# Norm chains of a two-layer diffusion trunk: additions and low parts on GpSimd, one function table for Ln and Exp, weight pieces split in halves

## The reference, cut to what matters

```python
def _rms_norm(x, g):
    xf = x.astype(jnp.float32)
    y = xf * lax.rsqrt(jnp.mean(xf * xf, axis=-1, keepdims=True) + EPS)
    return (y * g.astype(jnp.float32)).astype(x.dtype)

def _modulate(h, shift, scale):
    return h * (1 + scale) + shift
...
        h = _modulate(_rms_norm(x, norm_g[0]), sh1, sc1)
        hc = _modulate(_rms_norm(ctx, norm_g[0]), csh1, csc1)
...
        x = x + g1 * _rms_norm(y, norm_g[1])
        h2 = _modulate(_rms_norm(x, norm_g[2]), sh2, sc2)
        x = x + g2 * _rms_norm(ffn(h2), norm_g[3])
```

## Time and profile before

| | us |
|---|---|
| median of three runs | 1876.46 |
| lowest and highest | 1873.37 and 1878.36 |
| the profiled execution, its own time | 1877.49 |
| its span, first to last instruction | 1875.7 |
| TensorE, VectorE, ScalarE, GpSimd busy | 1744.5, 1080.5, 951.6, 0.2 |
| expert stage, first matmul to last | about 1032 to 1855 |

### The profile page before, as it was taken

The page is one execution under the profiler, slowest core; times in us unless marked ns, Lnnn a source line. Parts: engine busy times, 40 slices in busy tenths (PEclk is TensorE's granted clock), DMA queues, the critical chain, the costliest instruction groups (busy, mean ns, idle before and its releaser), DMA issues. The chain is left out here.

```text
span 1875.7 us, 22323 instructions
## 1 busy us (share of the span) xinstructions
PE 1744.5 (93%) x8560; PEld 1365.7 (73%) x8560; DVE 1080.5 (58%) x1076; ACT 951.6 (51%) x1037; POOL 0.2 (0%) x4
## 2 busy tenths in 40 slices
PE   6898999889999999699775999999999999999995
PEld 3685357458888788379564788888888888888884
DVE  2341332232222333453634798888888989899895
ACT  3513332352222222542454576767677777777774
POOL 0000000000000000000000000000000000000000
PEclk8898999889999999889986899999999999999997
DMA  7424374452222222132023698989899999999870
GB/s 274 194 90 170 106 263 160 180 198 90 94 108 90 90 95 107 37 107 79 40 94 131 245 367 327 367 324 368 339 353 346 348 348 345 353 340 375 320 307 24
DMA packets 56655, 403.05 MB, mean 215 GB/s; under 512 B 6288, under 2 KB 7568, under 8 KB 7952
## 3 DMA queue, kind: packets, MB, share of 16 engines
q1 hardware_dynamic: 56592, 402.17, 56.8%
HBM read 401.10 MB, written 1.05 MB: 214 GB/s over the span
## 5 line engine op out<-in xcount | busy, mean ns | idle before, releaser
L1114 DVE TENSOR_TENSOR wl<-raw,wh 128x2048 fp32r<-128x2048 f32 x269 | 615.7, 2292 | 101.1 <-ACT wh L670 100.9
L670 ACT ACTIVATE wh<-raw 128x2048 fp32r<-128x2048 f32 x269 | 515.3, 1917 | 150.9 <-PE ps L1198 150.9
L1196 PE MATMUL ps<-wh,ah 128*128 128x512 f32 (+1 forms) x808 | 314.2, 389 | 1.4 <-issue 1.4
L1198 PE MATMUL ps<-wh,al 128*128 128x512 f32 (+1 forms) x808 | 306.4, 379 | 0.0
L1196 PE MATMUL ps<-ah,wh 128*128 128x512 f32 (+1 forms) x736 | 285.5, 388 | 22.2 <-DVE al L764 14.3
L1197 PE MATMUL ps<-wl,ah 128*128 128x512 f32 (+1 forms) x808 | 305.3, 378 | 0.0
L1197 PE MATMUL ps<-al,wh 128*128 128x512 f32 (+1 forms) x736 | 277.9, 378 | 0.0
L1198 PE MATMUL ps<-ah,wl 128*128 128x512 f32 (+1 forms) x736 | 277.5, 377 | 0.0
L739 DVE TENSOR_TENSOR wl<-raw,wh 128x2048 fp32r<-128x2048 f32 x60 | 137.4, 2291 | 145.6 <-ACT wh L370 145.6
L1196 PEld LDWEIGHTS ps<-ah,wh 128*128 128x128 f32 x736 | 142.6, 194 | 58.2 <-issue 13.4
L1198 PEld LDWEIGHTS ps<-wh,al 128*128 128x128 f32 x808 | 152.6, 189 | 29.4
(11 more groups left out here) (217 smaller groups left out, 1727.6 us busy)
## 6 DMA issues: line engine op xcount, KB each, us to landing
raw<-in_w SPq DMA_DIRECT2D x377, 1024.0 KB, 4.8
x<-in_x SPq DMA_DIRECT2D x1, 2048.0 KB, 11.7
raw<-in_uq SPq DMA_DIRECT2D x1, 1152.0 KB, 5.7
raw<-in_ukv SPq DMA_DIRECT2D x1, 1024.0 KB, 7.8
out<-x SPq DMA_DIRECT2D x8, 128.0 KB, 1.9
raw<-in_dft SPq DMA_DIRECT2D x1, 512.0 KB, 3.7
cst<-in_cst SPq DMA_DIRECT2D x1, 320.0 KB, 12.0
rope<-in_rope SPq DMA_DIRECT2D x1, 256.0 KB, 7.0
```

The costliest lines, as they stand in the source:

```text
L670: act.activation(wh[:, J % SPLITS, :], slot(J % SLOTS), ACT.Copy).then_inc(w_hi, 1)
L1114: dve.tensor_tensor(wl[:, J % SPLITS, :], slot(J % SLOTS), wh[:, J % SPLITS, :].bitcast(F32), ALU.subtract).then_inc(w_lo, 1)
L1196: pe.matmul(out, lh, rh, start=start, stop=False)
L1198: return pe.matmul(out, ll, rh, start=False, stop=stop)
```

## The change

Four things change, and nothing else in the order of the work.

1. `residual`: VectorE makes source x scale x inverse root in one instruction per half (256 columns) into `tmp`; GpSimd adds `tmp` to x, one instruction per chunk. Chunk k waits until the addition of chunk k - 2 is done.
2. `modulate`: ScalarE scales only the latent half; VectorE scales the context half (`context_half`); ScalarE's copy waits for both; GpSimd subtracts to `al`. On VectorE `context_half` of chunk k - 1 is issued behind the multiplication of chunk k, and that one waits for the low part of chunk k - 2. O2, which has no context half, keeps its order.
3. `split`: each piece of 2048 columns outside the expert stage is copied and subtracted in two halves of 1024.
4. Function tables: one set that holds both Ln and Exp is loaded at three fixed places (after the first Silu, after the gate and up pieces, ahead of the last norm), and Silu's set once after the router's Exp.

```diff
+LN_EXP = "natural_log_exp_and_others"
...
-                    act.activation(wh[:, s % SPLITS, :], slot(ring_slot("main", s)), ACT.Copy).then_inc(w_hi, 1)
+                    for h in range(2):
+                        act.activation(wh[:, s % SPLITS, half(h)], slot(ring_slot("main", s))[:, half(h)], ACT.Copy
+                                       ).then_inc(w_hi, 1)
...
-                    for c in range(W // TL):
-                        act.activation(b[:, c * TL:(c + 1) * TL], b[:, c * TL:(c + 1) * TL], ACT.Identity,
-                                       bias=modv[:, shift + k, c:c + 1],
-                                       scale=scl[:, layer, which, k, c:c + 1]).then_inc(mod_h, 1)
+                    act.activation(b[:, 0:TL], b[:, 0:TL], ACT.Identity, bias=modv[:, shift + k, 0:1],
+                                   scale=scl[:, layer, which, k, 0:1]).then_inc(mod_h, 1)
                     if hi:
-                        act.wait_ge(mod_h, 2 * (KD * m + k + 1))
+                        act.wait_ge(mod_h, KD * m + k + 1)
+                        act.wait_ge(mod_c, KD * m + k + 1)
                         act.activation(ah[:, k, 0:W], b[:, 0:W], ACT.Copy).then_inc(mod_hi, 1)
...
+            act.preload_act_table_set(LN_EXP)
...
+            act.preload_act_table(ACT.Silu)
...
-                    dve.wait_ge(w_hi, s + 1)
-                    dve.tensor_tensor(wl[:, s % SPLITS, :], slot(ring_slot("main", s)), wh[:, s % SPLITS, :].bitcast(F32),
-                                      ALU.subtract).then_inc(w_lo, 1)
+                    for h in range(2):
+                        dve.wait_ge(w_hi, 2 * s + h + 1)
+                        ins = dve.tensor_tensor(wl[:, s % SPLITS, half(h)], slot(ring_slot("main", s))[:, half(h)],
+                                                wh[:, s % SPLITS, half(h)].bitcast(F32), ALU.subtract)
+                    ins.then_inc(w_lo, 1)
...
+            def context_half(b, layer, which, shift, k):
+                modv = (mod0, mod1)[layer]
+                dve.tensor_scalar(b[:, TL:T], b[:, TL:T], scl[:, layer, which, k, 1:2], modv[:, shift + k, 1:2],
+                                  op0=ALU.mult, op1=ALU.add).then_inc(mod_c, 1)
...
                     if k and dst is None:
                         j = chunks_before(n) + k - 1
-                        dve.wait_ge(mod_hi, KD * m + k)
-                        dve.tensor_tensor(al[:, k - 1, 0:W], tmp[j % 2][:, 0:W], ah[:, k - 1, 0:W].bitcast(F32),
-                                          ALU.subtract).then_inc(mod_lo, 1)
+                        dve.wait_ge(t_ready, j + 1)
+                        context_half(tmp[j % 2], layer, which, shift, k - 1)
...
                         if k >= 2:
                             dve.wait_ge(res_done, RES_BEFORE[n] + (W // TL) * (k - 1))
-                        normed(n, src(k), tmp[j % 2][:, 0:W], k)
-                    if k:
...
-                            dve.scalar_tensor_tensor(
-                                out=x[:, k - 1, c * TL:(c + 1) * TL], in0=tmp[j % 2][:, c * TL:(c + 1) * TL],
-                                scalar=scl[:, layer, which, k - 1, c:c + 1], in1=x[:, k - 1, c * TL:(c + 1) * TL],
-                                op0=ALU.mult, op1=ALU.add).then_inc(res_done, 1)
+                            ins = dve.scalar_tensor_tensor(
+                                out=tmp[j % 2][:, c * TL:(c + 1) * TL], in0=src(k)[:, c * TL:(c + 1) * TL],
+                                scalar=scl[:, layer, which, k, c:c + 1], in1=rinv[:, c * TL:(c + 1) * TL],
+                                op0=ALU.mult, op1=ALU.mult)
+                        ins.then_inc(t_ready, 1)
...
+        @block.gpsimd
+        def _(pool):
+            def low(m, k, src):
+                pool.wait_ge(mod_hi, KD * m + k + 1)
+                pool.tensor_tensor(al[:, k, :], src, ah[:, k, :].bitcast(F32), ALU.subtract).then_inc(mod_lo, 1)
...
+            def residual_add(n):
+                W = NORMS[n][1]
+                for k in range(KD):
+                    j = chunks_before(n) + k
+                    pool.wait_ge(t_ready, chunks_before(n) + k + 1)
+                    pool.tensor_tensor(x[:, k, 0:W], x[:, k, 0:W], tmp[j % 2][:, 0:W], ALU.add).then_inc(res_done, W // TL)
```

More of the change, by code:

```diff
@@ L244, in build @@
         mod_h, mod_hi, mod_lo, res_done = map(sem, ("mod_h", "mod_hi", "mod_lo", "res_done"))
-        mod_used = sem("mod_used")
+        mod_used, mod_c = sem("mod_used"), sem("mod_c")
         cond_ready, modv_ready, scales_ready = map(sem, ("cond_ready", "modv_ready", "scales_ready"))
@@ L283, in ring_landed, with half @@
             return landed[ring_slot(kind, i)], 16 * (RING_AT[kind, i] // EARLY_SLOTS + 1)
+        def half(h):
+            return slice(h * (PIECE // 2), (h + 1) * (PIECE // 2))
         def slot(n):
@@ L748, in normed, with modulate @@
                 dve.tensor_tensor(dst, src, rinv[:, 0:NORMS[n][1]], ALU.mult).then_inc(t_ready, 1)
-            def modulate(n, m, dst=None):
+            def context_half(b, layer, which, shift, k):
+                modv = (mod0, mod1)[layer]
+                dve.tensor_scalar(b[:, TL:T], b[:, TL:T], scl[:, layer, which, k, 1:2], modv[:, shift + k, 1:2],
+                                  op0=ALU.mult, op1=ALU.add).then_inc(mod_c, 1)
+            def modulate(n, m, layer=None, which=None, shift=None, dst=None):
                 K, W = NORMS[n]
@@ L770, in residual @@
                 inverse(n)
-                for k in range(K + 1):
-                    if k < K:
+                for k in range(K):
                         j = chunks_before(n) + k
@@ L831, in _ @@
             scale_pre(0, 0, 8).then_inc(scales_ready, 1)
+            dve.wait_ge(scales_ready, 1)
             for k in range(KD):
-                dve.wait_ge(mod_hi, k + 1)
-                dve.tensor_tensor(al[:, k, :], xn[:, k, :], ah[:, k, :].bitcast(F32), ALU.subtract).then_inc(mod_lo, 1)
+                dve.wait_ge(t_ready, k + 1)
+                context_half(xn[:, k, :], 0, 0, 0, k)
             def conv(c):
@@ L958, in _ @@
             residual(N_EY, lambda k: y_e[:, k, :], 0, 1)
-            modulate(N_E2, 1)
+            modulate(N_E2, 1, 0, 2, 24)
             dve.wait_ge(sem("mod_cols"), N_MOD)
@@ L991, in _ @@
             dve.memset(small[:, 9:10], 0.0).then_inc(sem("y2_used"), 1)
-            modulate(N_O1, 2)
+            modulate(N_O1, 2, 1, 0, 0)
             for p in range(10):
@@ L1028, in _ @@
             residual(N_OY, lambda k: y_o[:, k, :], 1, 1)
-            modulate(N_O2, 3, lambda k: h2f[:, k, :])
+            modulate(N_O2, 3, dst=lambda k: h2f[:, k, :])
             def two(at):
@@ L1112, in split_next @@
                     J = at.J + j
-                    dve.wait_ge(w_hi, PER_EXPERT * e + (MAIN + J + 1))
+                    dve.wait_ge(w_hi, PER_EXPERT * e + (2 * MAIN + J + 1))
                     dve.tensor_tensor(wl[:, J % SPLITS, :], slot(J % SLOTS), wh[:, J % SPLITS, :].bitcast(F32),
@@ L1189, in _, with modulated_low @@
             residual(N_OF, lambda k: acc[:, k, :], 1, 3)
+        @block.gpsimd
[3 more added lines that the diff above has]
+                pool.tensor_tensor(al[:, k, :], src, ah[:, k, :].bitcast(F32), ALU.subtract).then_inc(mod_lo, 1)
+            def modulated_low(n, m):
+                for k in range(KD):
+                    low(m, k, tmp[(chunks_before(n) + k) % 2])
+            def residual_add(n):
+                W = NORMS[n][1]
+                for k in range(KD):
+                    j = chunks_before(n) + k
+                    pool.wait_ge(t_ready, chunks_before(n) + k + 1)
+                    pool.tensor_tensor(x[:, k, 0:W], x[:, k, 0:W], tmp[j % 2][:, 0:W], ALU.add).then_inc(res_done, W // TL)
+            for k in range(KD):
+                low(0, k, xn[:, k, :])
+            residual_add(N_EY)
+            modulated_low(N_E2, 1)
+            residual_add(N_EF)
+            modulated_low(N_O1, 2)
+            residual_add(N_OY)
+            residual_add(N_OF)
         @block.tensor
@@ L1464, in _ @@
             sum_squares(N_O2)
-            pe.wait_ge(mod_h, 3 * 2 * KD + KD)
+            pe.wait_ge(mod_h, 3 * KD + KD)
             pe.wait_ge(root_ready, N_O2 + 1)
```

2 lines of the change are left out of this document (removed).

## The result

The kernel after takes 1880.99 us (median of 14 runs, 1877.79 to 1885.24); the kernel before, on the same chip, 1876.53 us (14 runs). The ratio is 1.0026, with a 95% interval from 1.0017 to 1.0034. That is 4.5 us slower by the medians, less than the 5.6 us that the prediction called "no change", but more than the measurement is uncertain. The profiled executions have spans of 1875.7 and 1880.3 us, so their traces can account for it: +4.6. One execution of all that are told of here stands apart and is in no ratio: one of the eleven of the kernel with one input took 6053.8 us.

A forecast was written before the change was run, and what follows sets the result against it. TensorE, busy 1744.5 of 1875.7 us, was taken as the bound, with wins or losses only where it waits. 18.8 + 2.3 + 9.7 - 25.4 - 2.7 = +2.7 us gave 1879 us; own range 1872 to 1886, 8 in 10 1863 to 1895.

The forecast's parts named there:

- Part 1: At the norms' roots: with Ln and Exp in one set a root has no table load, a gain of 25.4 us.
- EF, O1, OY, O2, OF: At these five roots nothing else goes on during the two loads: 2.57 us each, 12.8 us gained.
- the set's own three loads: Behind the first Silu, after the gate and up pieces, ahead of the last squares: ScalarE is idle there, so no cost.
- Q and KV: At these roots: Q gains 2.57 us, KV 0.8 of a possible 2.57 because of DMA, together 3.4.
- P: Time of one GpSimd pass over 512 columns, taken as 1.22 us; wrong as a whole if outside 1.0 to 1.4.
- rival B: GpSimd's pass is dearer, so slower: decides from 1.29 us per pass; 1894 us at 1.6, 1922 at 2.29; chance 0.24.
- Part 2: Modulates of E2 and O1: a closed loop of 2.98 us per chunk loses 18.8 us, the clock 2.3 more.
- The clock behind E2: After E2's modulate TensorE runs some 4.6 us at half speed, not having reached 2.4 GHz: 2.3 us lost.
- Part 3: Modulate of E1: the loop is open and GpSimd sets the pace at 1.25 us per chunk, a gain of 2.7 us.
- Part 5: Pieces in halves: zero; the split behind a modulate may hold the last low part by one half, 1.2 us at most.
- Part 4: Residuals, VectorE and GpSimd excluding each other: EF loses 4.9 us, OF and OY 2.2 each, EY 0.4; 9.7 in all.
- A: In the residuals VectorE and GpSimd work side by side: 10.8 us less than forecast, 1868 us, a gain; chance 0.25.

The follow-up runs named there:

- the kernel with one input: The kernel before with only the GpSimd residuals, the inverse-root multiplication left out so VectorE reads one SBUF input: 1876.94 us, ratio 1.0001.
- The opened order: The kernel after with VectorE's context half of chunk k - 1 issued ahead of chunk k's wait and multiplication in E2 and O1: 1869.98 us, ratio 0.9963.
- tables and E1: The kernel before with the table loads and the new modulate in E1 alone, everything else as before: 1858.93 us, ratio 0.9900.

## Why the prediction was right, and where it was off

The time, 1881 us, is 2 us from the forecast, and the loop in E2 and O1 costs what it was said to. By the prediction's own steps:

- **Part 1, the tables: too large by 6 us** (25.4 forecast, 19.3 alone). The first step that failed is the line "EF, O1, OY, O2, OF: nothing else goes on. 2 x 1.283 = 2.57 us each". I read the loads as lying between the last sum and the first multiplication. But ScalarE issues the first load as soon as its last square is done; TensorE's sum runs at the same time, and the Ln waits for it in any case. The changed kernel shows it as idle time ahead of the Ln: 1.22 us in EF and O1, 0.79 in O2 and OF, 0.42 in EY and OY. The five roots gave about 8.5 us by the shifts instead of 12.8. The second is "the set's own three loads lie where ScalarE has nothing to do": the one behind the gate and up pieces costs 1.4. With the tables alone the clock at the start of the expert stage took 1.7 more (0.57 from 1031 to 1035). A load of 2.66 us, as the Trainium skill (ScalarE: Activation LUTs, What ACT_TABLE_LOAD costs) has it with its drain, is further off still: 22 loads fewer gave 19.3 us. Q and KV gave 3.3 with the tables alone, as forecast, but 1.4 in the changed kernel; 1.3 of the difference is the clock at Q's sums. E1's root gains 1.6 after the wait for DMA at 38.59 (2.0 forecast), and the last modulation piece of E2 waits for its load as said.

```profile
773.31 0.69 ACT L395 ACTIVATE rinv<-ps,eps 128x512 f32<-128x512 f32 x1 [1.22 <-PE ps L1249]
```
```profile
38.59 1.93 PE L1268 MATMUL ps<-raw 128*32 128x256 f32 x16 [3.87 <-DMA raw<-in_w]
...
380.70 1.07 PE L1268 MATMUL ps<-raw 128*32 128x256 f32 x16 [1.84 <-DMA raw<-in_w]
```

- **The pass, P**: 1.22 chosen, 1.27 measured, just below the point (1.29) from which rival B was to decide. With VectorE beside it the pass of EF takes 1.37, above that point. The estimate of 1.12, a quarter of the figure in the Trainium skill (GPSIMD Engine Reference, Performance versus the Vector engine), was further off than the 1.22.
- **Part 2, the loop**: right in place and in size. The period is 3.11 us (2.98), a modulate 22.5 us (23.4: the last low part comes 1.23 us behind the one ahead of it, since no multiplication stands between the last two context halves). The opened order proves the cause. The clock behind E2 cost 1.1 us, not 2.3: TensorE is at the lower level all through the chain, as said, but is back at 2.4 GHz within the window 404 to 408.

```profile
390.00:400.00 10.00, 4.95 (x9) 2.49 (x9) 3.05 (x6) 3.45 (x7) 4.45 (x4) 0.50 0.01 2
404.00:408.00 4.00, 4.00 (x13) 3.03 (x12) 3.12 (x4) 2.39 (x3) 0.65 (x1) 0.64 0.00 0
408.00:412.00 4.00, 4.00 (x20) 3.30 (x19) 0.00 (x0) 0.00 (x0) 0.00 (x0) 1.00 0.73 262
```

- **Part 3, E1**: 1.3 us in the chain instead of 2.7. Eight passes take 11.34 us, but that is not 1.42 for each. Seven start 1.29 us apart (1.25 forecast), the first four while VectorE makes the context halves, and the eighth takes 2.30: VectorE has begun half a weight piece's subtraction just ahead of it. Part 5 had named this hold, "by one half, 1.2 us at most", and left it out of the sum; it cost 1.0. With whole pieces (tables and E1) the eighth pass starts ahead of the subtraction and takes 1.28, and the subtraction is the one held, 2.65 us for 2.28. That run shows no gain at its end from E1, most of it lost to the clock. I had priced it as pure gain.

```profile
47.43 11.34 POOL L1210 TENSOR_TENSOR al<-raw,ah 128x512 fp32r<-128x512 f32 x8 [46.98 <-ACT ah L412]
```
```profile
56.42 1.23 DVE L749 TENSOR_TENSOR wl<-raw,wh 128x1024 fp32r<-128x1024 f32 x1 [4.78 <-ACT wh L375]
```
```profile
56.47 2.30 POOL L1210 TENSOR_TENSOR al<-raw,ah 128x512 fp32r<-128x512 f32 x1
```

- **Part 4, the residuals**: 9.7 forecast, 5.6 alone, 8.8 when taken from the changed kernel. The engines do exclude each other, so A is refuted; the size was off because the first instruction of a pair falls into the time in which GpSimd waits for its data anyway. VectorE in EF, one pair:

```profile
777.40 1.88 DVE L792 SCALAR_TENSOR_TENSOR raw<-raw,scl,rinv 128x256 f32<-128x256 f32 x2
```
  The pass at 777.62 begins in the middle of the first instruction and ends at 778.99; the second instruction comes behind it, and its 0.4 us and the pass make the 1.80. EY cost 0.3 with the residuals alone, as forecast (0.4), but 2.7 beside the other three parts; which of them brings that out stays open.
- **Part 5, halves**: nothing clear of the noise when alone, as said, but for the hold in E1 above.
- **The expert stage**, priced at nothing, took 2.0 us more. Its first products ran slower: the granted clock fell in the kernel after, and not before (where the same window has 1.00) nor in the kernel with the old residuals:

```profile
1050.00:1054.00 4.00, 1.74 (x8) 1.12 (x6) 2.63 (x3) 3.52 (x4) 0.00 (x0) 1.00 0.01 2
1054.00:1058.00 4.00, 3.99 (x13) 3.22 (x14) 3.81 (x3) 1.24 (x2) 0.00 (x0) 0.68 0.80 274
```
  TensorE was busy for 1.74 of the 4 us ahead of the fall. The tables alone have a low window there too (0.57 from 1031 to 1035). The kernel with the old residuals was busy for 2.24 of 4 in the like place (1040.13 to 1044.13) and stayed at 1.00. Which small shift decides it stays open.

Part by part, each alone against its forecast: the tables +6.1 us, the modulates +2.2 (20.6 for 18.4), the halves +1.5, the residuals -4.1. That is +5.7; the whole is 3.5 below the sum of its parts, within their intervals, and so 2.2 above the forecast. The mechanism of the largest term, the loop, was right. That the time was met to 2 us is partly luck: the 6 of the tables and the 4 of the residuals cancelled for the most part.

## What to carry to other kernels

A load, or anything an engine can issue ahead of its wait, costs only what sticks out behind the thing waited for: look at what the next instruction waits for before pricing it in full, and check that the place it is moved to is idle. When work is moved to another engine, walk the loop through every queue and every buffer; with two buffers and an instruction queued behind a wait, three engines can be slower than two. And before VectorE and GpSimd are set to work side by side, see that VectorE's second stream comes from PSUM: here that, with a place for each chunk and whole pieces, turned a loss of 5 us into a gain of 27, 19 of which the tables give alone. And before a shift between two timelines is put down to a wait, look at the granted clock of the stretch: here it moved single stages by 1.3 to 1.7 us.

## What the runs showed of the hardware that was not expected

- A GpSimd pass held small VectorE instructions with two SBUF inputs as well: over 16 columns they take 0.17 us alone, and took 1.17 and 1.21 us beside a low part.

```profile
402.26 1.17 DVE L819 TENSOR_TENSOR scl<-mod,vec 128x16 f32<-128x16 f32 x1
403.47 1.21 DVE L813 SCALAR_TENSOR_TENSOR scl<-mod,vec 128x16 f32<-128x16 f32 x1
404.71 0.17 DVE L819 TENSOR_TENSOR scl<-mod,vec 128x16 f32<-128x16 f32 x1
```
- The hold goes both ways, though GpSimd's share is small: 1.37 us for a pass instead of 1.27, 0.90 instead of 0.72.
- A multiplication that reads one of its two inputs from PSUM is not held (0.69 us, the same as alone), and writing the root to PSUM cost ScalarE nothing (0.60 us against 0.63).
